# A gather ring for expert rows: five slots of 12 KB in place of four of 16 KB, the row's stored number fetched ahead of the slot wait, and the row's V part added in its own step

## The reference, cut to what matters

```python
def _peer(h, w_q, keys, u_tab, v_tab):
    ...
        gate = jax.nn.softmax(best_s, axis=-1)
        u = jnp.take(u_tab, idx, axis=0)
        act = jax.nn.gelu(jnp.einsum('thkd,td->thk', u, hb).astype(jnp.float32), approximate=False)
        w = (gate * act).astype(hb.dtype)
        return jnp.einsum('thk,thkd->td', w, jnp.take(v_tab, idx, axis=0))
...
        x = x + _peer(h2, peer_w_q[l], peer_keys[l], peer_u[l], peer_v[l]).reshape(B, S, D)
    return _rmsnorm(x, final_norm_g)
```

## Time and profile before

| | before |
|---|---|
| median of 3 runs | 4404.04 us |
| lowest and highest | 4399.64 and 4413.66 us |
| the profiled execution's own time | 4409.72 us |
| its span | 4407.9 us |
| mean granted TensorE clock | 0.933 |
| TensorE busy | 3741.6 us (85%) |
| VectorE busy | 2771.1 us (63%) |
| ScalarE busy | 920.9 us (21%) |
| GpSimd busy | 1195.4 us (27%) |
| HBM read | 1465.82 MB |
| GpSimd's DMA queue | 948.08 MB, 53.6% of 16 engines' span |
| longest in the chain that ended last | TensorE 56%, DMA 29%, VectorE 8% |

### The profile page before, as it was taken

The page is one execution under the profiler, slowest core; times in us unless marked ns, Lnnn a source line. Parts: engine busy times, 40 slices in busy tenths (PEclk is TensorE's granted clock), DMA queues, the critical chain, the costliest instruction groups (busy, mean ns, idle before and its releaser), DMA issues.

```text
span 4407.9 us, 39729 instructions
## 1 busy us (share of the span) xinstructions
PE 3741.6 (85%) x13406; PEld 2225.7 (50%) x13406; DVE 2771.1 (63%) x4163; ACT 920.9 (21%) x2049; POOL 1195.4 (27%) x768
## 2 busy tenths in 40 slices
PE   9999999999999999576799997899987776556565
PEld 3444499447666676464688873543433332111111
DVE  3232377005999999956666677856567687555555
ACT  2133211101222211231111211111112222222222
POOL 0000000000233322322133332332234444444444
PEclk9999999999999999888999998999998888877878
DMA  3111168888999999999999999999999999999998
GB/s 131 58 59 66 67 212 303 313 300 325 396 405 405 392 398 410 376 398 394 422 414 415 417 419 427 418 428 427 410 381 369 354 366 348 359 364 346 349 345 322
DMA packets 162491, 1488.36 MB, mean 338 GB/s; under 512 B 24512, under 2 KB 24640, under 8 KB 33344
## 3 DMA queue, kind: packets, MB, share of 16 engines
q0 software_dynamic: 81408, 948.08, 53.6%
q1 hardware_dynamic: 70704, 512.44, 29.8%
q10 hardware_dynamic: 10256, 26.35, 1.5%
HBM read 1465.82 MB, written 20.97 MB: 337 GB/s over the span
## 4 chain that ended last, share of the span: by engine, by line
PE 56%; DMA 29%; DVE 8%; issue 6%; POOL 1%; ACT 1%; POOLq 0%; SPq 0%; ACTq 0%; DVEq 0%
PE bank L1818 32%; DMA arena_c<-in_peer_uv_rest,arena_c 15%; PE bank L2149 6%; PE bank L1869 5%; PE bank L1922 5%; DMA wring<-in_peer_u_tiles 4%; DMA wring<-in_w_in 4%; DVE arena_o L1461 3%; DMA arena_c<-in_peer_uv,arena_c 3%; PE bank L1966 2%; PE bank L1884 1%; PE bank L2008 1%; DVE arena_o L1705 1%; POOL cols L687 1%; DVE arena_c L1448 1%
## 5 line engine op out<-in xcount | busy, mean ns | idle before, releaser
L1818 PE MATMUL bank<-arena_h,wring 128*128 128x128 f32 (+5 forms) x6784 | 1406.9, 370 | 66.1 <-DMA wring<-in_peer_w_q 22.7
L679 POOL DMA_INDIRECT arena_c<-in_peer_uv,arena_c x272 | 662.4, 2435 | 2609.1 <-DVE arena_o L1461 1531.9
L1818 PEld LDWEIGHTS bank<-arena_h,wring 128*128 128x128 f32 x6784 | 1047.0, 195 | 423.6 <-issue 133.1
L1461 DVE SCALAR_TENSOR_TENSOR arena_o<-arena_c,arena_o 128x2048 f32<-128x2048 f32 (+1 forms) x384 | 782.6, 2038 | 221.2 <-ACT arena_c L863 162.2
L1448 DVE SCALAR_TENSOR_TENSOR arena_c<-arena_c 128x2048 f32<-128x2048 f32 (+1 forms) x384 | 759.0, 1977 | 178.4 <-DMA arena_c<-in_peer_uv_rest,arena_c 141.2
L2179 PE MATMUL bank<-arena_c,arena_h 128*128 128x512 f32 x508 | 339.8, 805 | 238.4 <-ACT arena_h L1051 237.5
L2149 PE MATMUL bank<-wring,arena_h 128*128 128x512 f32 x1024 | 445.0, 594 | 16.5 <-DMA wring<-in_peer_u_tiles 16.5
L2179 PE MATMUL bank<-arena_c,cols 128*128 128x512 f32 x448 | 277.1, 752 | 164.7 <-ACT cols L1025 164.5
L687 POOL DMA_INDIRECT cols<-dots,cols x240 | 240.1, 1000 | 508.6 <-DVE arena_o L1461 229.5
L2179 PEld LDWEIGHTS bank<-arena_c,arena_h 128*128 128x128 f32 x508 | 110.2, 240 | 468.0 <-ACT arena_h L1051 380.7
L859 ACT ACTIVATE arena_c<-arena_c 128x1 f32<-128x1 f32 x272 | 55.1, 203 | 1384.6 <-DVE arena_c L1448 1369.7
(11 more groups left out here) (239 smaller groups left out, 2848.2 us busy)
## 6 DMA issues: line engine op xcount, KB each, us to landing
wring<-in_w_in SPq DMA_DIRECT2D x176, 1024.0 KB, 10.4
wring<-in_peer_u_tiles SPq DMA_DIRECT2D x64, 1024.0 KB, 17.0
wring<-in_w_out SPq DMA_DIRECT2D x48, 1024.0 KB, 8.8
wring<-in_peer_w_q SPq DMA_DIRECT2D x48, 1024.0 KB, 11.1
wring<-in_gla_w_o SPq DMA_DIRECT2D x32, 1024.0 KB, 10.4
wring<-in_conv_w_pw SPq DMA_DIRECT2D x32, 1024.0 KB, 12.6
wring<-in_w_v SPq DMA_DIRECT2D x16, 1024.0 KB, 4.9
wring<-in_w_ga SPq DMA_DIRECT2D x16, 1024.0 KB, 5.0
```

What stands on the lines that cost most here:

```text
L679: pool.indirect_dma_start(out=slot_of(n), out_offset=None, in_=uv_tab, in_offset=column(idx_cur, U % 2, k)).then_inc(landed(n)[0], 16)
L1461: V.scalar_tensor_tensor(dst, by_tile(row), act_w[:, k:k + 1], dst, ALU.mult, ALU.add).then_inc(row_used, 1)
L1818: last = M(ps[bank][:, at:at + hi - lo], w_tile(slot)[:, k, :], act_in[:, k, lo:hi], start=k == 0, stop=k == KT - 1)
```

## The change

- Half rows get a ring of their own: `SLOTS2` = 5 slots of 12 KB (3072 numbers) in the memory of the four slots of 16 KB. `slot_of`, `landed` and the new `v_part` find a row's slot, its semaphore and its V part; `lies_over(n)` names the last row that lay where row n goes, across the border between the two rings too.
- The number's gather is issued before the slot's wait, on semaphores of its own (`a_ready`, 6 of them in turn). ScalarE waits on this semaphore before the GELU (`picked`); VectorE's dot product waits for the row alone.
- VectorE adds row n's V part at the end of step n, behind the top-k part, for half rows as for whole rows.
- Block 3 goes through the same loops as block 2: the second set of functions and buffers is gone on POOL, ScalarE, VectorE and TensorE, and its hardware loops are written out. The final norm's pieces and block 2's closing copy hang on step numbers of the one loop. In block 3 the next unit's indices are copied at step `COPY3_AT` = 8, as before.
- ScalarE's diagonal matrices wait for TensorE's sum of four rows back, as before; only the count is written in another way.

Cut to its core:

```diff
-STEPS = SIDE * TOP
+STEPS = UNITS * TOP
+BLOCK3 = SIDE * TOP
 HALF = D // 2
 ROW2 = HALF + D
 EXPERTS = NK * NK
 PITCH = EXPERTS
+SLOTS2 = 5
+AHEAD = 6
...
-CLOSE_AT, LAST_CLOSE_AT = 0, 1
+CLOSE_AT = BLOCK3 + 1
+COPY3_AT = TOP // 2
...
         def slot_of(n):
-            return uv_row[n % SLOTS]
+            if n < WHOLE:
+                return uv_row[n % SLOTS]
+            return view(arena_c, RU + (n - WHOLE) % SLOTS2 * ROW2, ROW2)
+
+        def v_part(n, first, count):
+
+            at = D if n < WHOLE else HALF
+            return slot_of(n)[:, at + first * 512:at + (first + count) * 512]
 
         def landed(n):
 
-            whole = min(n + SLOTS, WHOLE) // SLOTS if n >= WHOLE else n // SLOTS + 1
-            halves = (n - WHOLE) // SLOTS + 1 if n >= WHOLE else 0
-            return uv_ready[n % SLOTS], 16 * whole + 32 * halves
-
-        HAD = 16 * (WHOLE // SLOTS) + 32 * ((STEPS - WHOLE) // SLOTS)
-
-        idx_cur2 = view(arena_c, SG + 1760, 2, TOP).bitcast(U32)
-
-        diag = view(arena_h, 2 * D, SLOTS, P)
-        act_u2 = view(arena_h, 2 * D + 512, 2, TOP)
-        act_g2 = view(arena_h, 2 * D + 544, 2, TOP)
-        act_w2 = view(arena_h, 2 * D + 576, 2, TOP)
+            if n < WHOLE:
+                return uv_ready[n % SLOTS], 16 * (n // SLOTS + 1)
+            s, turn = (n - WHOLE) % SLOTS2, (n - WHOLE) // SLOTS2 + 1
+            return uv_ready[s], 16 * turn + (16 * WHOLE // SLOTS if s < SLOTS else 0)
+
+        def picked(n):
+
+            return a_ready[(n - WHOLE) % AHEAD], 16 * ((n - WHOLE) // AHEAD + 1)
+
+        def lies_over(n):
+
+            if n < WHOLE:
+                return n - SLOTS
+            return n - SLOTS2 if n >= WHOLE + SLOTS2 else WHOLE - SLOTS + min(n - WHOLE, SLOTS - 1)
...
-            def half_row(idx, idx_a, m, k, s):
-                pool.indirect_dma_start(out=act_a[:, k:k + 1], out_offset=None, in_=dots_flat,
-                                        in_offset=column(idx_a, m, k)).then_inc(uv_ready[s], 16)
-                pool.indirect_dma_start(out=uv_row[s][:, 0:ROW2], out_offset=None, in_=uv2_tab,
-                                        in_offset=column(idx, m, k)).then_inc(uv_ready[s], 16)
-
-            for U in range(WHOLE_UNITS, SIDE):
+            for U in range(WHOLE_UNITS, UNITS):
                 pool.wait_ge(idx_ready, U + 1)
                 for k in range(TOP):
                     n = U * TOP + k
-                    pool.wait_ge(row_used, n + 1)
-                    pool.wait_ge(sum_used, n - WHOLE + 1)
-                    half_row(idx_cur, idx_dot, U % 2, k, n % SLOTS)
-
-            with pool.Fori(0, PH // 2) as i:
-                for m in range(2):
-                    hold(pool, idx2_ready, i * 2 + (m + 1), pool_passed)
-                    for k in range(TOP):
-                        n = m * TOP + k
-                        hold(pool, row_used, i * 2 * TOP + (STEPS + n + 1), pool_passed)
-                        hold(pool, sum_used, i * 2 * TOP + (STEPS - WHOLE + n + 1), pool_passed)
-                        half_row(idx_cur2, idx_dot2, m, k, n % SLOTS)
+                    pool.indirect_dma_start(out=act_a[:, k:k + 1], out_offset=None, in_=dots_flat,
+                                            in_offset=column(idx_dot, U % 2, k)).then_inc(picked(n)[0], 16)
+                    pool.wait_ge(row_used, SLOTS + lies_over(n) + 1)
+                    if lies_over(n) >= WHOLE:
+                        pool.wait_ge(sum_used, lies_over(n) - WHOLE + 1)
+                    pool.indirect_dma_start(out=slot_of(n), out_offset=None, in_=uv2_tab,
+                                            in_offset=column(idx_cur, U % 2, k)).then_inc(landed(n)[0], 16)
...
+                    there, value = picked(U * TOP + k)
+                    act.wait_ge(there, value)
...
-                    act.wait_ge(sum_used, s - WHOLE + 1)
+                    if s - SLOTS >= WHOLE:
+                        act.wait_ge(sum_used, s - SLOTS - WHOLE + 1)
...
-                    dst, row = block_of(x2, b)[:, KT // 2:], slot_of(n)[:, D:ROW2]
+                    dst, row = block_of(x2, b)[:, KT // 2:], v_part(n, 2, 2)
...
+            for U in range(UNITS):
...
-                    if s > WHOLE:
-                        add_row(s - 1)
                     beside(s)
+                    if s == CLOSE_AT:
+                        close_block2()
+                    for blocks, first in (([0, 1], BLOCK3), ([2], BLOCK3 + 2 * TOP)):
+                        if s == first + SUMS_AT + 1:
+                            final_means(blocks)
+                        if s == first + SCALE_AT:
+                            dve.wait_ge(gbc_in, 64)
+                            final_scale(blocks)
                     for part in topk:
                         part(k)
-                    if k == COPY_AT:
-                        if U < SIDE - 1:
-                            indices(U + 1)
-                        else:
-                            indices2(0, SIDE)
-                    if s < WHOLE and not takes:
+                    if U < UNITS - 1 and k == (COPY_AT if U < SIDE else COPY3_AT):
+                        indices(U + 1)
+                    if s < STEPS - 1 and not takes:
                         add_row(s)
-            add_row(STEPS - 1)
...
-            def add_half(n):
-
-                dve.wait_ge(act2_done, 2 * n + 2)
-                dve.wait_ge(row_used, STEPS + n + SLOTS)
-                dst = x2[:, KT // 2:, (NB - 1) * P:NB * P]
-                V.scalar_tensor_tensor(dst, by_tile(uv_row[n % SLOTS][:, D:ROW2]),
-                                       act_w2[:, n // TOP % 2, n % TOP:n % TOP + 1], dst, ALU.mult, ALU.add)\
-                    .then_inc(row_used, 1)
...
-            def sums(bank, weights, s, count, stop):
-
-                for q in range(count):
-                    last = M(ps[bank + q][:], weights, uv_row[s][:, HALF + q * 512:HALF + q * 512 + 512],
-                             start=False, stop=stop)
-                return last
+            def sums(n):
+
+                for q in range(2):
+                    last = M(ps[(4 if n < BLOCK3 else 0) + q][:], diag1[:, n % SLOTS, :], v_part(n, q, 1),
+                             start=False, stop=n in (BLOCK3 - 1, STEPS - 1))
+                    if n == STEPS - 1:
+                        last.then_inc(fin_bank, 1)
+                if n < STEPS - 1:
+                    last.then_inc(sum_used, 1)
...
+                if s == BLOCK3:
+                    pe.wait_ge(s_ev, 2 * 3 * PH)
+                    residual(3, 0)
                 pe.wait_ge(diag1_ready, s - WHOLE + 1)
-                sums(4, diag1[:, s % SLOTS, :], s % SLOTS, 2, s == STEPS - 1).then_inc(sum_used, 1)
+                sums(s)
```

More of the change, by code:

```diff
@@ L496, in hybrid_block @@
         mix1_free = sem("mix1_free")
[L497 to L499 removed]
+        uv_ready = [sem(f"uv_ready{s}") for s in range(SLOTS2)]
+        a_ready = [sem(f"a_ready{s}") for s in range(AHEAD)]
         sum_used = sem("sum_used")
@@ L1641, in parts_at, with close_block2, final_means, final_scale @@
                 return after
-            for U in range(SIDE):
+            def close_block2():
+                dve.wait_ge(sum_used, BLOCK3 - WHOLE)
+                for q in range(2):
+                    ins = V.tensor_copy(x2[:, 4 * q:4 * q + 4, 2 * P:3 * P], by_tile(ps[4 + q][:]))
+                ins.then_inc(mix1_free, 1)
+                dve.wait_ge(mix1_free, 1)
+            def final_means(blocks):
+                for b in blocks:
+                    dve.wait_ge(fin_sum, b + 1)
+                    mean_square(52 + b, 48 + b, D).then_inc(fin_ms, 1)
+            def final_scale(blocks):
+                for b in blocks:
+                    dve.wait_ge(fin_root, b + 1)
+                    chain.step(inverse(60 + b, 56 + b))
+                    if b == 2:
+                        dve.wait_ge(out_done, 32)
+                    V.scalar_tensor_tensor(by_tile(y_ready[b]), block_of(x2, b), small[:, 60 + b:61 + b],
+                                           by_tile(gbc_f), ALU.mult, ALU.mult).then_inc(fin_y, 1)
+            for U in range(UNITS):
                 topk = []
@@ L2206, in _ @@
                     head_scores(U + 2, 0, NB2, qh2)
-            def last_products(i, ends):
-                for n in range(2 * TOP):
-                    s, end = n % SLOTS, ends and n == 2 * TOP - 1
-                    pe.wait_ge(diag_ready, i * 2 * TOP + (n + 1))
-                    if not end:
-                        sums(0, diag[:, s, :], s, 2, False).then_inc(sum_used, 1)
-                        continue
-                    for q in range(2):
-                        M(ps[q][:], diag[:, s, :], uv_row[s][:, HALF + q * 512:HALF + q * 512 + 512],
-                          start=False, stop=True).then_inc(fin_bank, 1)
-            pe.wait_ge(s_ev, 2 * 3 * PH)
-            residual(3, 0)
-            with pe.Fori(0, (UNITS - SIDE) // 2 - 1) as i:
-                last_products(i, False)
```

(1 more changed line is left out.)

125 lines of the change are left out of this document (25 added, 100 removed).

## The result

The changed kernel takes 4253.26 us, the median of 4 runs between 4248.0 and 4257.05, against 4408.68 for the kernel before in the same comparison: a ratio of 0.9649, 95% interval 0.9627 to 0.9671 (below, too, a ratio stands with its interval). It is faster, as forecast, and by 1.6 times as much: 155 us in place of 95.

The account below looks back on a forecast made before the run. The half-row stage (1097 us) was taken as bound by its slot ring; 974 us of transfers, 4 of start and 24 of VectorE loss made 1002, 95 less, so 4309 us, range 4255 to 4369.

Parts of the forecast that it names:

- the ring: Half-row slots: three rows a turn of 13.87 us bound the stage; five rows in 17.7 would leave transfers as bound.
- What the transfers then give: Half-row stage: 389.8 MB at 400 GB/s, taken between 379 and 413, would need 974 us.
- the 24 us of loss charged to VectorE: Block 2, units 17 to 22: long top-k parts delay slots, 4 us a unit for six units.
- The window of the first half rows: From 3302 to 3316 us, four half rows queued at once: 413 GB/s, taken as the upper bound.
- The lower bound: Half-row transfers: busy share counts true work, only the idle 6 to 7% can be filled, giving 379 GB/s.
- only the idle time: Rival for the half-row stage: transfers reach just 379 GB/s, 53 us less, 4351 us; chance 0.16.
- Start and parts: Half-row stage: 4 us until the queue is full, plus 24 us for VectorE's top-k parts in block 2.
- hidden at 3.3 us a row: GpSimd in half rows: two gathers and pauses take at most 3.3 us, below the transfers' 3.93 us a row.
- TensorE gives the slot back last: Half-row ring: TensorE's four matmuls end a slot's use, 6.2 us after the row's landing.
- the sign that was given: In the profile after, GpSimd's row gather would wait for TensorE more often than for VectorE.
- The limit of 358 GB/s: Rule behind a rival: HBM share per core already binds half rows, so nothing is gained, 4404 us; chance 0.07.
- The slower rival: VectorE's wait for ScalarE becomes the bound from 2.2 us a step; at 3 us, 176 us more, 4580; chance 0.05.

Follow-up runs that it names:

- without the number: The changed kernel without the number's gather, so the table's half of the dot product is missing from the GELU's input: 4233.6 us, ratio 0.9617.
- the run that was to give them back earlier: The changed kernel with VectorE's adding directly behind the dot product, ahead of the top-k part: 4274.5 us, ratio 0.9705.
- the memset: The changed kernel with one GpSimd memset of 128 x 512 numbers ahead of each number's gather: 4261.3 us, ratio 0.9685.
- three memsets: The changed kernel with three GpSimd memsets of 128 x 512 numbers ahead of each number's gather: 4507.7 us, ratio 1.0244.
- three slots: The changed kernel with three slots of 12 KB in place of five, early number and own-step adding kept: 4465.4 us, ratio 1.0130.
- the step alone: The changed kernel with four slots and the number's gather behind the slot's waits; own-step adding stays: 4379.2 us, ratio 0.9944.
- the number alone: The changed kernel with four slots and the adding behind the next row's product; the early number stays: 4296.7 us, ratio 0.9751.
- the late adding: The changed kernel with the adding put back behind the next row's product; five slots and early number stay: 4253.1 us, ratio 0.9659.
- the slots alone: The changed kernel with adding behind the next product and number behind the slot's waits; five slots stay: 4258.0 us, ratio 0.9664.

## Why the prediction was wrong

The mechanism held in the main: the ring was the bound, its three rows a turn are seen in the chains of waits, the transfers became the bound, landing went from 9.1 to 12.7 us (11 to 13 forecast), the share to 1.01 (0.98 or more), and the adding waits 0.69 us a step in block 3 (0.7). What failed are two sizes of the sum: the 400 GB/s of "What the transfers then give", above all, and the 24 us of loss charged to VectorE. The stage was to take 1002 us and took 948.

- **The rate, 42 of the 54 us.** I took 400 GB/s between bounds of 379 and 413. The steady rate is 417 to 418, above the upper bound; 389.8 / 400 - 389.8 / 418 = 42 us. The window of the first half rows should have been taken as it stood, and not as the top: its last 2 us, at 381 GB/s, were already back at the shallow queue, and the ten from 3304 to 3314 us moved 419. The lower bound, and with it the rival "only the idle time", rested on the DMA share as a count of true work. It is none: the share is 0.93 at 350 GB/s and 1.00 at 401 and at 408, 1.01 at 418 and at 426. From 350 to 426 the rate rises by 22%, the share by 9%. What shrinks is the time that a 12 KB packet counts as busy: 517 ns before, 472 in the changed kernel, 464 without the number. So part of a packet's busy time is waiting (what for, isn't shown), and a share near 1 doesn't say that the engines can give no more.
- **The loss in block 2, 12 of the 54 us.** Start and parts were charged 4 + 24 = 28 us; the stage's 389.6 MB at 418 GB/s take 932 us, which leaves 16 of 948 for both. VectorE's load was rightly seen as near the bound. Whether late slots cost what is left isn't shown: the run that was to give them back earlier made VectorE the bound instead.
- **9 us outside the stage**, the scatter of what runs ahead of it, make up the rest: 54 + 9 = 63 is the distance of the profiled execution (4251.5) from the 4314.7 forecast for it.
- **GpSimd** was called hidden at 3.3 us a row, since one dot product a row can hold one gather up. In fact the adding holds up the other: the row's gather that starts at 3911.81, under the adding of 3911.38, takes 1.67 us. The two gathers and pauses come to 3.7 of 3.77 us. The step's result stands, as the memset shows, and three memsets bring the rival to life. That GpSimd is no bound came out right, the sum for it did not.
- **TensorE gives the slot back last**: shown for three slots, and in block 2 of the changed kernel (26 waits against 19). In block 3 the sign that was given fails: 1 wait of the row's gather for TensorE, 6 for VectorE. There a slot hardly matters any more, and the four matmuls take 1.99 us at a granted clock of 0.95, not 3.78 at 0.80.
- **The two blocks**: about 490 and 515 us were forecast. Cut at 3740 us the stage gives 498 for block 3 and 450 for block 2, where the loss of 24 us was charged on top of the rate.
- **The change's parts**: the prediction priced only their sum. It counted the own-step adding as one of the two rows that the turn gains. Beside the fifth slot it is worth nothing, since four rows a turn fill the transfers already.
- **The limit of 358 GB/s**, which the Trainium skill gives (DMA: Bandwidth & Descriptors, section "Where 436 GB/s comes from"), didn't hold on this core: 418 GB/s over 300 us, and 426 without the number. The slower rival didn't come either: VectorE's wait for ScalarE in the step is 0.69 us, not 2.2.

Open: the step alone and the number alone have about the same mean of rows in the queue (9.9 / 4.41 and 8.7 / 3.95, 2.2 each), yet 359 and 401 GB/s. In the timeline of the first the row gathers come in bunches, two of them 8.7 us apart:

```profile
4019.74 0.94 POOL L703 DMA_INDIRECT arena_c<-in_peer_uv_rest,arena_c  x1 [0.30 <-issue]
...
4027.24 0.94 POOL L701 DMA_INDIRECT cols<-dots,cols  x1 [6.57 <-DVE arena_o L1436]
...
4028.49 1.30 POOL L703 DMA_INDIRECT arena_c<-in_peer_uv_rest,arena_c  x1 [0.30 <-issue]
```

The traces bear this out in part: counted from the end of its gather to its landing, a single row was under way in 23% of the 300 us with the step alone, and in 4% with the number alone. But in the first the stretches with a single row moved about as much as those with two (346 and 355 GB/s), so bunching isn't shown to be all of the difference. No version that computes the whole result beats the changed kernel: the late adding (4253.1) and the slots alone (4258.0) are level with it.

## What to carry to other kernels

Where buffers form a ring around transfers, write down the turn: landing, work until the last reader lets go, issue; divide by the buffers that are really in the turn. What every turn holds (a second small gather ahead of the large one) costs its time over the number of rows in a turn. A further buffer can make all such parts worthless at once, so price them together and not in a sum. Take the ceiling of the transfers from a stretch in which several are queued, and not from the busy share.

## What was not expected of the hardware

- The DMA share reaches 1.00 at 401 GB/s, while the same traffic still goes to 418 with a deeper queue.
- A gather of 128 numbers of 4 bytes beside each row costs 2% of the rate: 426 to 418 GB/s, 18 to 20 us for 240 rows. Only a quarter of that is its own packets' time (22 of some 90 ns a row on each engine).
- A gather of GpSimd that starts under VectorE's product (1.23 us) or its adding (1.28) takes up to 1.67 to 1.79 us in place of 0.94. In the rows above it ends 0.8 us behind that instruction (3911.50 behind 3910.69, 3913.48 behind 3912.66). Put elsewhere by a memset ahead of it, the same gather takes 0.98.
- TensorE's granted clock in block 3 is 0.95, against 0.80 before, though its busy share is lower (277 of 498 us against 343 of 582); the share is lower in part because the same matmuls take less time at that clock. From 3900 to 4200 us the clock is 0.73 to 0.84 in the runs that move 317 to 359 GB/s, and 0.95 to 0.99 in those at 408 and above. Why it rises with the pace isn't shown.
